# A decoder layer on one core: new orders at its begin, at the end of its linear attention, in its merge and in its FFN, and stored rows loaded in place

## What is computed

```python
h = rmsnorm(x, norm1)
proj = h @ w_in        # 12 query, 4 key, 4 value heads | GLA q, k, v, out-gate | low rank (16) | gates A, B
oa = dilated_attention(rope(rmsnorm(qa)), rope(rmsnorm(ka)), va)       # 3 groups (window, dilation)
log_a = log_sigmoid(ab @ w_a_up + b_a) / 16
ob = rmsnorm(gla(qb, kb, vb, log_a), gn_b) * silu(rb)                  # S_t = diag(a_t) S_{t-1} + k_t^T v_t
y = sigmoid(ga) * (oa @ w_proj_a) + sigmoid(gb) * (ob @ w_proj_b)
x = x + y @ w_out
x = x + (silu(h2 @ w_ffn_gate) * (h2 @ w_ffn_up)) @ w_ffn_down         # h2 = rmsnorm(x, norm2)
```

## Time and profile before

| | |
|---|---|
| median of 3 runs | 1797.01 us (1796.91 to 1797.05) |
| profiled execution | 1796.22 us |
| its span, first to last instruction | 1794.6 us |
| TensorE busy | 1756.4 us, 98% |
| VectorE, ScalarE, GpSimd busy | 1084.8, 718.2, 479.0 us |
| memory read, written | 150.88, 44.45 MB |
| mean granted TensorE clock | 0.999 of full speed |

### The profile page before, as it was taken

The page is one execution under the profiler, slowest core; times in us unless marked ns, Lnnn a source line. Parts: engine busy times, 40 slices in busy tenths (PEclk is TensorE's granted clock), DMA queues, the critical chain, the costliest instruction groups (busy, mean ns, idle before and its releaser), DMA issues.

```text
span 1794.6 us, 26674 instructions
## 1 busy us (share of the span) xinstructions
PE 1756.4 (98%) x9186; PEld 1494.5 (83%) x9186; DVE 1084.8 (60%) x1927; ACT 718.2 (40%) x1645; POOL 479.0 (27%) x574
## 2 busy tenths in 40 slices
PE   6999999999999999999999999999999999999999
PEld 6888888888889888898978888778888888878887
DVE  4363554745538767584966545785555555566876
ACT  5335353353444443544462133543323333244443
POOL 3010101110026151523310000045655665420210
PEclk9999999999999999999999999999999999999999
DMA  7222322424122111020245232223322323288674
GB/s 212 73 52 71 105 69 85 110 70 110 61 87 73 48 36 59 24 70 18 88 151 178 82 118 82 106 88 112 117 88 99 111 88 111 100 296 300 225 242 161
DMA packets 169810, 196.38 MB, mean 109 GB/s; under 512 B 9552, under 2 KB 119472, under 8 KB 169216
## 3 DMA queue, kind: packets, MB, share of 16 engines
q1 hardware_dynamic: 157904, 165.23, 28.8%
q0 software_dynamic: 5552, 19.65, 3.4%
q10 hardware_dynamic: 6272, 10.49, 1.6%
HBM read 150.88 MB, written 44.45 MB: 109 GB/s over the span
## 4 chain that ended last, share of the span: by engine, by line
PE 77%; issue 11%; DVE 7%; POOL 4%; ACT 1%; DMA 1%; SPq 0%; POOLq 0%; DVEq 0%; ACTq 0%
PE bank L2351 18%; PE bank L2353 18%; PE bank L2352 18%; PE lvl_ps L2353 5%; PE lvl_ps L2351 5%; PE lvl_ps L2352 5%; PE bank L2435 2%; POOL dbuf L871 1%; POOL dbuf L870 1%; PE bank L2461 1%; DVE fbuf L1860 1%; PE bank L2447 1%; PE lvl_ps L2486 1%; DVE fbuf L1861 1%; PE lvl_ps L2542 1%
## 5 line engine op out<-in xcount | busy, mean ns | idle before, releaser
L2351 PE MATMUL bank<-act_hi,w_hi 128*128 128x512 f32 x568 | 227.8, 401 | 0.3 <-ACT gbuf L1100 0.3
L2353 PE MATMUL bank<-act_hi,w_lo 128*128 128x512 f32 x568 | 221.7, 390 | 0.0
L2352 PE MATMUL bank<-act_lo,w_hi 128*128 128x512 f32 x568 | 221.1, 389 | 0.0
L2351 PE MATMUL bank<-ca,wq 128*128 128x512 f32 x528 | 206.3, 391 | 7.6 <-DVE wq L2096 5.2
L2353 PE MATMUL bank<-ca,wq 128*128 128x512 f32 x528 | 205.5, 389 | 0.0
L2352 PE MATMUL bank<-ca,wq 128*128 128x512 f32 x528 | 205.5, 389 | 0.0
L2351 PE MATMUL bank<-w_hi,act_hi 128*128 128x256 f32 (+1 forms) x576 | 180.6, 314 | 3.6 <-DVE act_lo L1629 3.6
L2353 PE MATMUL bank<-w_hi,act_lo 128*128 128x256 f32 (+1 forms) x576 | 177.5, 308 | 0.0
L2352 PE MATMUL bank<-w_lo,act_hi 128*128 128x256 f32 (+1 forms) x576 | 177.3, 308 | 0.0
L2351 PEld LDWEIGHTS bank<-act_hi,w_hi 128*128 128x128 f32 x568 | 106.8, 188 | 22.8 <-issue 1.3
L2353 PEld LDWEIGHTS bank<-act_hi,w_lo 128*128 128x128 f32 x568 | 106.6, 188 | 22.9
(11 more groups left out here) (371 smaller groups left out, 4187.3 us busy)
## 6 DMA issues: line engine op xcount, KB each, us to landing
w_raw<-in_w_in SPq DMA_DIRECT2D x60, 512.0 KB, 4.7
rawd<-in_w_ffn_down SPq DMA_DIRECT2D x99, 256.0 KB, 5.0
rx<-y_scratch SPq DMA_DIRECT2D x77, 256.0 KB, 4.3
wr<-in_w_ffn_gate SPq DMA_DIRECT2D x11, 1024.0 KB, 5.3
wr<-in_w_ffn_up SPq DMA_DIRECT2D x11, 1024.0 KB, 5.4
y_scratch<-sq SPq DMA_DIRECT2D x11, 1024.0 KB, 4.3
y_scratch<-yq SPq DMA_DIRECT2D x33, 256.0 KB, 2.0
gate_scratch<-gbuf ACTq DMA_DIRECT2D x32, 256.0 KB, 2.1
```

The source lines that it names most:

```text
L2351: pe.matmul(ps, lhs_hi, rhs_hi, start=first, stop=False, skip_group_check=onto)
L2352: pe.matmul(ps, lhs_hi, rhs_lo, start=False, stop=False, skip_group_check=onto)
L2353: return pe.matmul(ps, lhs_lo, rhs_hi, start=False, stop=last, skip_group_check=onto)
```

## The change

Begin: SP loads two tiles of x, the value weight in four pieces of two row blocks by all 512 columns, then the other six tiles. TensorE first runs twelve matmuls of the identity by itself. It turns tiles 0 and 1 (`turn_pair`), runs the value products of these two, column block by column block, each when its operands are split, turns tiles 2 and 3 ahead of the last block, and does the same for these; tiles 4 to 7 are turned in halves (`turn_half`), and every value group is one tile by 512 columns. The low-rank product comes last.

Heads: the gate moves from step 4 to step 6, the second multiplication by the merge weights of the first head too, and GpSimd's fourth group of differences ahead of the store. In the last head the state products of chunks 4 to 6 go first, into banks 0 and 1 (`last_kv`), the states of chunks 6 and 7 get their own place (`last_state`), and the first merge product is cut into blocks for both token halves (`both_halves`).

Stored rows: `oa_hi` and `oa_lo` become two halves of one tensor `oa`. The oa rows keep the stage slots, and the six ob rows are loaded into `act_lo` itself, once the last projection product has read it, and split there.

Merge: the order of sigmoids, casts and splits at its start, and its third gate product ahead of the last piece of `wout`.

FFN: a new order at the start, two operand sums cut in halves, `ca` slots renamed; at the end the last product stands behind the first step of the down projection, the last multiplications and sums move from GpSimd to DVE, and TensorE's wait at the end of each group is gone, ACT waiting for `dprod` instead (`step_done`).

```diff
@@ begin, SP and PE
         def load_v(i):
-            sp.dma_start(w_raw[:, i, :].rearrange("p (kt n) -> p kt n", n=P),
-                         w_in[:, :, C_V + P * i:C_V + P * i + P]).then_inc(raw_in[i], 16)
+            sp.dma_start(w_raw[:, i, :].rearrange("p (kt n) -> p kt n", n=HALF),
+                         w_in[:, 2 * i:2 * i + 2, C_V:C_V + HALF]).then_inc(raw_in[i], 16)
...
-            if i == 3:
-                load_v(0)
-                load_v(1)
-        load_v(2)
-        load_v(3)
+            if i == 1:
+                for k in range(4):
+                    load_v(k)
...
+        for _ in range(WARM):
+            pe.matmul(banks[0][:, 0:P], ident[:, :], ident[:, :], start=True, stop=True)
+        turn_pair(0)
+        for q in range(2):
+            for kt in range(NK):
+                if q == 0 and kt % 2 == 0:
+                    pe.wait_ge(lo_done, kt // 2 + 1)
+                pe.wait_ge(nt_lo, NK * q + kt + 1)
+                if q == 0 and kt == NK - 1:
+                    turn_pair(1)
+                if q == 1 and kt == NK - 2:
+                    turn_half(range(4))
+                for j in (2 * q, 2 * q + 1):
+                    mm = value(j, kt)
+                    if kt == NK - 1:
+                        mm.then_inc(st_ready, 1)
+        turn_half(range(4, NK))
+        for j in range(4, NT):
+            pe.wait_ge(st_evac, j - 2)
@@ heads, POOL and DVE
-                work = ["O4", "O5", "d0", "O6", "d1", "O7", "d2", "G0", "d3"] + last
+                work = ["O4", "O5", "d0", "O6", "d1", "O7", "d2", "d3", "G0"] + last
...
-                if tail and s == 4:
+                if tail and s == 6:
                     dve_gate(h - 1)
@@ last head, PE
+        for c in (4, 5, 6):
+            pe.wait_ge(kh_evac, 8 * (H - 1) + c + 1)
+            pe.matmul(last_kv_ps(c), khat[:, c, :], vtok[:, c, :], start=True, stop=True).then_inc(last_kv, 1)
         last_m(4)
         pe_t(H - 1, 3)
         last_m(5)
         last_m(6)
+        pe.wait_ge(lo_done, C0 + 1)
+        pe.wait_ge(state_done, 8 * (H - 1) + 7)
+        both_halves(0, [0], oa_hi, oa_lo, 0, (0, 1), H)
         last_m(7)
@@ stored rows, SP
-            src = oa_d[i] if i < H else ob_d[i - H]
             alone(sp)
-            sp.dma_start(stage[:, i % 4, :], src).then_inc(stage_in[i % 4], 16)
+            if i < H:
+                sp.dma_start(stage[:, i, :], oa_d[i]).then_inc(stage_in[i], 16)
+            else:
+                sp.dma_start(act_lo[:, i - H, :].bitcast(F32), ob_d[i - H]).then_inc(ob_in[i - H], 16)
...
         sp.wait_ge(ob_out, 16 * (H - 1))
+        sp.wait_ge(st_ready, 2 * B0 + 2 * TB * H)
         for i in range(4, N_ST):
-            sp.wait_ge(stage_lo, i - 3)
             load_output(i)
+        load_m(3)
@@ merge, DVE
                 for kt in range(4):
                     m = N_MT + kt
+                    if kt == 3:
+                        merge(it, 2)
@@ end of the FFN, PE
-        pe.wait_ge(evac, 5 * NPAIR - 1)
-        product(NPAIR - 1, 1, 6).then_inc(prod, 2)
...
             if kt < FK - 1:
                 mm.then_inc(prod, 1)
-            else:
-                pe.wait_ge(dprod, 4 * q + 4)
-                pe.sem_inc(prod, 1)
+
+        down_step(0)
+        pe.wait_ge(evac, 5 * NPAIR - 1)
+        product(NPAIR - 1, 1, 6).then_inc(prod, 1)
+        for n in range(1, NSTEP):
+            down_step(n)
```

509 lines of the change are left out of this document (298 added, 211 removed).

## The result

The changed kernel takes 1771.13 us (median of 4 runs, 1771.09 to 1771.33), the kernel before 1796.96 (4 runs, 1795.33 to 1797.05). The ratio is 0.986, with an interval of 0.9848 to 0.9872. The profiled execution took 1771.15 us and its span is 1769.5, so 25.1 us of span went. TensorE is busy for 1754.1 us of it.

A forecast was written before the change was run, and what follows sets the result against it. TensorE was taken as the bound, working 1756.4 of 1794.6 us. Terms 10.0 + 2.8 + 3.2 + 0.7 + 3.8 + 3.0 = 23.5 us off 1796.2 give 1772.7, plus 0.8 for the median 1773.5; range 1769.5 to 1780.

The forecast's parts named there:

- forecast case: Whole kernel: all six terms come near their size, 1770 to 1777 us; chance 0.58.
- Begin: Start of the kernel, value stage: new load order and products tile by tile save 10.0 us (6 to 12).
- a stretch at 0.50: Start of the kernel: one three-us stretch at the 1.2 GHz clock level was assumed, costing 1.4 us.
- Rival 2: Start of the kernel runs at 1.2 GHz to about 26 us: 8 to 9 us more, 1782; chance 0.15.
- Heads: Linear attention heads: moving the gate and merge multiplication later removes four level-mask waits, 2.8 us (0 to 2.8).
- merge: Merge: third gate product ahead of the last weight piece removes a TensorE wait, 0.7 us (0 to 0.7).
- Tail: Last linear-attention head: state products first, projection blocks between chunks; 3.2 us saved (1 to 4), 0.9 of waits left.
- The stored rows: Last head's six rows loaded in place: the load change costs and gains nothing on TensorE, cover 0.4 us.
- FFN start: Start of the FFN: VectorE's reordered work lets the thirteenth product start sooner, 3.8 us (0 to 4.5).
- FFN end: End of the FFN: 1.0 us at the last product, 2.0 at group ends, together 3.0 us (1 to 3.4).
- rival 4: Slower: granted clock stays at 0.50; through the whole begin it would give some 1807 us; chance 0.02.
- Rival 1: FFN's start stays put and the heads' waits move to the next mask: 3.8 and half of 2.8 fail, 1778.7; chance 0.12.

The follow-up runs named there:

- the slots: Changed kernel with the six stored rows of the linear attention loaded through the four stage slots again, gates' loads between the fourth and fifth: 1776.35 us.
- the early copy: Changed kernel with ScalarE's copy of `p1b` for the third pair moved ahead of three casts that wait for GpSimd's differences: 1770.20 us.
- the two faster versions: Changed kernel with ScalarE's `p1b` copy ahead of three casts, 1770.20 us; the same plus VectorE's sum for the FFN's thirteenth product made sooner, 1770.02 us.

## Why the prediction was right, and where not

The forecast was 1773.5 with 1769.5 to 1780, the measured time is 1771.13. The forecast case had 1770 to 1777, so it is the one that came. The sum of terms was 23.5 for 25.1, but it was closer than its terms:

- **Begin** (10.0, measured 10.2). The first product stood at 10.90, as worked out. Two steps failed and cancelled. The second weight piece was taken to land at 9.8; ScalarE could cast it only at 11.73 (row below), VectorE idled 1.67 us, and the first two tiles were done at 24.64 instead of 23.5. Against that, the 1.4 us for a stretch at 0.50 did not come. The rest (44.0 forecast, 44.1 measured) held. The begin spreads by 1.5 us from execution to execution, so that 10.2 stands so near 10.0 is in part luck.

```profile
11.73 1.05 ACT L1041 CAST w_hi<-w_raw 128x1024 fp32r<-128x1024 f32 x1 [1.31 <-DMA w_raw<-in_w_in]
```

- **Rival 2** (1.2 GHz to about 26 us) fell. From its first entry at 7.44 us on the granted clock is 1.00, the products from 10.90 on stand 0.23 us apart, and TensorE's gaps behind its first work are 0.70 and 0.67 us. With four tiles of x first and a gap of 5.98 there is the stretch at 0.50. The prediction's sentence that the trace shows the lower level only behind the gap misread the 1.00 ahead of the first entry: in the kernel before the first transposes, from 12.96 to 15.8, went at that pace too.
- **Heads** (2.8, 3.45) and **merge** (0.7, 1.2): the mechanism was right, the step that failed is the price of a stop. "About 0.1" for the restart was too little. A listed 0.79 cost 1.1, four listed waits of 2.9 cost 3.9, and a stop with 0.30 listed cost 0.55. In the heads the four waits gave 3.8 between the two traces, and the spread at the first turned output took 0.3.
- **Tail** (3.2, 4.2). Forecast were 0.9 us of waits in place of the old ones; there is none, since the forecast for VectorE's reduction and splits was too late. Of the 4.2 us 2.3 are the order of the state products. The stored rows were not late, as forecast, but the reason given for their worth was wrong: see the slots.
- **FFN start** (3.8, 1.5). This is the term that failed. The count of VectorE's work held to the last instruction: 34 operations of 512 columns, the sum for the thirteenth product as the last of them, and ten of 1024 stand behind the norm of the last tile. They took 33.3 us (1134.92 to 1168.22) where the forecast had 31.6 and 0.7 for waits: two of 1024 stand 2.28 apart, so 1.14 each and not 1.1, VectorE stood for 0.74 us once, and there are smaller holes. The product came at 1168.27, that is 21.8 us sooner and not 20.5, because 19.05 were won already; its own share is 2.8 of the forecast 3.8. The comparison also had a flaw: in the kernel before the sum was done at 1189.07, 1.0 us ahead of the thirteenth product, since the stops stood ahead of the eleventh and twelfth. So VectorE's sum bounds this product only now. The sum before and after:

```profile
1188.39 0.68 DVE L2122 TENSOR_TENSOR sg<-bank,ps 128x512 f32<-128x512 f32 x1
...
1167.54 0.68 DVE L2177 TENSOR_TENSOR sg<-bank,ps 128x512 f32<-128x512 f32 x1
```

The step that was missing is what comes behind it. The sum stopped at the thirteenth product, and the third product behind it now waits 1.43 us for `p1b`, where that wait was 0.28 before. That gave 1.3 back, and the early copy shows it.

- **FFN end** (3.0, 4.55). 1.26 for the last product (forecast 1.0), 3.3 for the groups (forecast 2.0), both again the price of a stop. By the prediction's own prices, 0.3 and 0.1, six stops are 2.4; its 2.0 is a slip, and so is the 1807 of rival 4, which by its own figures (58 us of work in about 100) would be some 1815.
- **Rival 1** came in part: the FFN's start gave 2.3 us less than forecast, by another mechanism, but the waits in the heads did not move on.

The clock also fell in the changed kernel, at a place that nobody had named:

```profile
1161.50:1163.00 1.50, 1.50 (x5) 1.21 (x4) 1.35 (x3) 1.50 (x3) 0.00 (x0) 0.50 0.00 0
```

It is 0.50 behind the wait of 1.83 us at 1159.86, for 3.4 us. It costs nothing: the thirteenth product waits for VectorE, and stands 8.41 us behind the wait in this trace, and 8.42 in the trace with four tiles of x first, where the clock stayed at 1.00 there and the listed wait is 2.71 instead of 1.10. In the kernel with the wait between groups the stretch at 0.50 fell behind the second wait, from 1170 to 1173, and took the place of the wait for `p1b`. Of the thirteen traces of the changed kernel and its edits it fell behind the first of the two waits in five, behind the second in five and not at all here in three, and apart from the three kernels with the early copy the FFN's start takes 415.7 to 416.0 us whichever it is. So a wait that a trace lists may be shortened by a slow stretch ahead of it.

**What stays open.** Why the increment behind a wait costs 0.2 us was not taken apart. The 0.1 us between the two faster versions can't be told from these runs, and against the changed kernel, whose runs are not of the same set, the gain of 1.7 us rests on the traces; the medians differ by 0.9. The new order of VectorE at the FFN's start and the merge's order were not put back by themselves; their shares, 1.5 and 1.2 us, are read from the two traces. In three traces (both without the identity matmuls, and the one with GpSimd's multiplications) 0.8 to 0.9 us is lost in the tenth step of the down projection, at 1580 to 1583. In the first of them ScalarE waits there 4.41 us for a load of down weights, and 3.27 in the changed kernel; no run was made for it.

## What to carry to other kernels

Price a stop by the starts of the matmuls around it, less the running pitch, and not by the idle time that the profile lists; a stop that is not listed at all can cost a third of a microsecond, and an increment behind it adds to that. When a wait is removed at an engine that is the bound, follow the waiting engine past the first place that the sum reaches, to each operand of the next products. A load that is hidden in the old order has to be costed in the new one, since the time at which its data is wanted moves with everything else.

## What the runs showed of the hardware

- TensorE's first matmuls run at half the pace: 0.21 us for a transpose that takes 0.11 later. The change comes with the first entry of the granted clock in the trace (7.44, 11.14 and 15.82 us in three kernels); the 1.00 that a view shows ahead of it is no measurement. In the changed kernel the identity matmuls take this on themselves; the profile records the twelve as 24, in 4.89 us.
- Behind a stop the granted clock fell to 0.50 in some executions and not in others: it did after 5.98 us, after 1.90 behind a stop of 0.62, after 1.83 in the changed kernel and after 2.69 in the kernel with the wait between groups, and it did not after 1.80 and 2.71 at the same two places in the kernel with four tiles of x first. It lasted 3.4 us, and 6.8 behind the 5.98.
- VectorE's subtraction of two SBUF operands of 512 columns takes 0.68 us, and 1.78 beside GpSimd.
- A wait with a semaphore increment behind it stops TensorE for 0.55 us, the wait alone for 0.35.
